# Negated decay sums as the exponential's bias, two directions added ahead of one product, and z and turned outputs in two PSUM banks

## The reference

```python
A_cum = jnp.cumsum(A, axis=-1)
scores = jnp.einsum("bclhn,bcshn->bhcls", Cc, Bc) * jnp.exp(segsum(A))
y_diag = jnp.einsum("bhcls,bcshp->bclhp", scores, xd)
...
y = (y_f + y_b).reshape(b, L, D_SSD)
y = rmsnorm(y * jax.nn.silu(z.astype(F32)), ssd_norm_w)
```

## Time and profile before

| | |
|---|---|
| runs shown | 953.66, 953.76, 956.06 us; median 953.76 |
| profiled execution, its own time | 954.61 us |
| its span, first to last instruction | 952.8 us |
| PE busy in the span | 855.1 us (90%) |
| DVE, POOL, ACT busy | 401.3, 210.1, 162.7 us |

### The profile page before, as it was taken

One profiled execution on the slowest core, in us unless ns is written; L12 is line 12 of the kernel. 1 busy time (PEld: TensorE's weight loads), 2 busy tenths in 40 slices (PEclk: granted clock), 3 DMA queues, 4 the chain that ended last, 5 costly groups with the idle time before them and its releaser, 6 DMA issues.

```text
span 952.8 us, 18676 instructions
## 1 busy us (share of the span) xinstructions
PE 855.1 (90%) x8036; PEld 483.1 (51%) x8036; DVE 401.3 (42%) x773; ACT 162.7 (17%) x369; POOL 210.1 (22%) x255
## 2 busy tenths in 40 slices
PE   1899999999899999999999994699998999999940
PEld 1656655555554555564444442455554555555520
DVE  1430012644664589985323265632222322222227
ACT  4121001212222222221010012011111111111113
POOL 0169999600141333330000000100000000000022
PEclk9999999999899999999999997699999999999985
DMA  9942755880310000069200004399999999998427
GB/s 349 419 171 90 274 223 212 290 312 1 133 44 1 1 1 1 0 239 337 115 22 23 9 14 147 142 381 419 390 415 397 352 401 379 406 404 334 152 75 279
DMA packets 41809, 198.91 MB, mean 209 GB/s; under 512 B 6848, under 2 KB 16256, under 8 KB 24704
## 3 DMA queue, kind: packets, MB, share of 16 engines
q1 hardware_dynamic: 22032, 162.82, 43.2%
q0 software_dynamic: 6224, 22.55, 6.8%
q10 hardware_dynamic: 13472, 12.37, 4.1%
HBM read 175.66 MB, written 22.05 MB: 208 GB/s over the span
## 4 chain that ended last, share of the span: by engine, by line
PE 57%; DVE 9%; DMA 3%; issue 2%; POOL 1%; ACT 1%; ACTq 0%; DVEq 0%; POOLq 0%
PE bank L928 19%; PE bank L796 14%; PE bank L941 9%; PE bank L660 6%; DMA slot_out<-yT 2%; PE bank L918 2%; PE bank L933 1%; PE bank L698 1%; DVE ex L1629 1%; DVE xs L1682 1%; DVE xs L2009 1%; POOL ex L1436 1%; DVE ex L1645 1%; PE bank L762 1%; DMA ex<-slot_out,ri 1%
## 5 line engine op out<-in xcount | busy, mean ns | idle before, releaser
L588 PE MATMUL bank<-hT,ring 128*128 128x512 f32 (+1 forms) x640 | 178.4, 438 | 1.5 <-DMA ring<-w_ring 1.5
L588 PEld LDWEIGHTS bank<-hT,ring 128*128 128x128 f32 x640 | 95.8, 192 | 72.0 <-issue 69.8
L1930 DVE TENSOR_TENSOR bcT<-bcT,bank 128x128 f32<-128x128 f32 x51 | 14.6, 287 | 166.4 <-ACT bcT L1255 166.4
L660 PE MATMUL bank<-ring,hT 128*128 128x512 f32 x160 | 76.9, 617 | 4.5 <-DVE ex L1653 2.2
L928 PE MATMUL bank<-ex,yT 128*32 128x256 f32 x1216 | 75.8, 392 | 1.2 <-ACT yT L1265 1.2
L928 PE MATMUL bank<-ring,yT 128*32 128x256 f32 x1248 | 76.5, 387 | 0.0
L796 PE MATMUL bank<-ring,yT 128*128 128x512 f32 x160 | 70.9, 593 | 0.8 <-DVE yT L1691 0.8
L1444 POOL DMA_INDIRECT yT<-h_dram,token_of x16 | 15.5, 969 | 237.2 <-PE bank L918 220.2
L1436 POOL TENSOR_TENSOR ex<-ex,dts 128x512 f32<-128x512 f32 x40 | 44.3, 1106 | 101.6 <-ACT ex L1167 101.5
L928 PEld LDWEIGHTS bank<-ex,yT 128*32 128x32 f32 x1216 | 37.6, 113 | 28.1 <-issue 3.4
L928 PEld LDWEIGHTS bank<-ring,yT 128*32 128x32 f32 x1248 | 38.4, 111 | 26.3 <-issue 2.2
(11 more groups left out here) (311 smaller groups left out, 1228.0 us busy)
## 6 DMA issues: line engine op xcount, KB each, us to landing
ex<-w_exp SPq DMA_DIRECT2D x36, 1024.0 KB, 18.0
ring<-w_exp SPq DMA_DIRECT2D x36, 1024.0 KB, 15.7
ring<-w_ring SPq DMA_DIRECT2D x13, 2048.0 KB, 11.6
yT<-w_late SPq DMA_DIRECT2D x16, 1024.0 KB, 6.6
hT<-w_exp SPq DMA_DIRECT2D x12, 1024.0 KB, 15.8
uT<-w_exp SPq DMA_DIRECT2D x12, 1024.0 KB, 18.2
slot_out<-ex POOLq DMA_DIRECT2D x13, 512.0 KB, 16.7
ex<-x SPq DMA_DIRECT2D x5, 512.0 KB, 8.3
```

What stands on the lines that cost most here:

```text
L588: mm = pe.matmul(o, w[:, k, (f % 4) * P:(f % 4 + 1) * P], hT[:, k, lo:hi], start=(k == 0), stop=(k == KT - 1))
L660: mm = pe.matmul(psb[6][:, :], hT[:, k, j * P:(j + 1) * P], w[:, k, :], start=(k == 0), stop=(k == KT - 1), skip_group_check=True)
L1930: tt(ab[v % 2], sg[v % 2], psb[v % 2][:, P:2 * P], ALU.mult).then_inc(s_ac, 1)
```

## The change

Three edits. The products of L741 go: instead, ten small products ahead of z of group 0 put all negated sums into bank 7, ACT copies them to `ncum`, and the exponential of each 128 columns takes its column of `ncum` as a per-partition bias, so that one exponential of 512 columns becomes four of 128. DVE adds the two directions first (256 columns) and multiplies the sum by C·B (256 columns). z of group jg goes to bank 6 or 7 by turns, and so do the turned outputs; z of group jg then waits for the silu of jg-2, or, from group 4 on, for the copy of the turned outputs of jg-4. `turn_y` of group jg moves behind `diagonal(4jg+7)`, into PE's step 4jg+10, and DVE's copy of it moves to behind its step 4jg+8. The first part of the output projection waits for the copies and the silus that used its bank.

```diff
--- before.py
+++ after.py
@@ -230,6 +230,14 @@
         def out_bank(j, hf_, c):
 
             return psb[6] if (j, hf_, c) == (0, 0, 1) else psb[2 * c + hf_]
+
+        def z_bank(jg):
+
+            return psb[6 + jg % 2]
+
+        def turn_bank(jg):
+
+            return psb[7] if jg >= 2 * NJ - 3 else psb[6 + jg % 2]
 
         def pooled_banks(i):
 
@@ -303,6 +311,7 @@
         s_sout = sem("context_states_stored")
         s_wd = sem("decays_times_dt")
         s_e = sem("exponents_built")
+        s_nc = sem("negated_sums_copied")
         s_ex = sem("decays_exponentiated")
         s_w = sem("scores_decayed")
         s_dg = sem("diagonal_products")
@@ -654,10 +663,14 @@
                 w = ring[:, m % RING, :].rearrange("p (k c) -> p k c", k=KT)
                 if ks[0] == 0 and jg < 2:
                     pe.wait_ge(s_ring[m % RING], 16 * (m // RING + 1))
-                if ks[0] == 0 and jg >= 1:
-                    pe.wait_ge(s_zs, jg)
+                if ks[0] == 0 and jg == 1:
+                    pe.wait_ge(s_nc, 1)
+                if ks[0] == 0 and 2 <= jg < 4:
+                    pe.wait_ge(s_zs, jg - 1)
+                if ks[0] == 0 and jg >= 4:
+                    pe.wait_ge(s_yT, jg - 3)
                 for k in ks:
-                    mm = pe.matmul(psb[6][:, :], hT[:, k, j * P:(j + 1) * P], w[:, k, :],
+                    mm = pe.matmul(z_bank(jg)[:, :], hT[:, k, j * P:(j + 1) * P], w[:, k, :],
                                    start=(k == 0), stop=(k == KT - 1), skip_group_check=True)
                 if ks[-1] == KT - 1:
                     mm.then_inc(s_z, 1)
@@ -726,6 +739,11 @@
                     pool_product(n + 2)
             pe.wait_ge(s_st, 5)
             pe.wait_ge(s_u, 8)
+            for d in range(2):
+                for j in range(NJ):
+                    c = j * 32 + d * H
+                    pe.matmul(psb[7][:, c:c + H], tabT[d][:, j * P:(j + 1) * P], nstackb[:, d * H:(d + 1) * H],
+                              start=True, stop=True)
             project_z(0, range(KT))
 
 
@@ -735,12 +753,6 @@
                 if i >= 2:
                     pe.wait_ge(s_ex, i - 1)
                 pe.matmul(o[:, :], idb[:, :], MASK4, start=True, stop=False, skip_group_check=True)
-                o4 = o[:, :].rearrange("p (h d t) -> p h d t", h=2, d=2)
-                for d in range(2):
-                    c = d * H + hh
-                    pe.matmul(o4[:, :, d, :], tabT[d][:, j * P:(j + 1) * P],
-                              nstackb[:, c:c + 2].unsqueeze(2).to_broadcast([96, 2, P]), start=False, stop=False,
-                              skip_group_check=True)
                 for q in range(4):
                     h, d = hh + q // 2, q % 2
                     c = d * H + h
@@ -775,11 +787,12 @@
 
             def turn_y(jg):
                 pe.wait_ge(s_yc, jg + 1)
-                if jg >= 1:
+                pe.wait_ge(s_zs, min(jg + 3, 2 * NJ))
+                if jg >= 2 * NJ - 2:
                     pe.wait_ge(s_yT, jg)
                 for q in range(4):
                     k = 4 * (jg % 2) + q
-                    mm = pe.transpose(psb[7][:, q * P:(q + 1) * P], xs[:, jg // 2, k * P:(k + 1) * P], ident)
+                    mm = pe.transpose(turn_bank(jg)[:, q * P:(q + 1) * P], xs[:, jg // 2, k * P:(k + 1) * P], ident)
                 mm.then_inc(s_ytr, 1)
 
 
@@ -809,14 +822,15 @@
                 if NS - 3 <= i < NS + 1:
 
                     if i == NS - 3:
-                        pe.wait_ge(s_zs, 2 * NJ)
+                        pe.wait_ge(s_zs, 2 * NJ - 1)
+                        pe.wait_ge(s_yT, 2 * NJ - 3)
                     project_part(0, 0, 1, range(2 * (i - NS + 3), 2 * (i - NS + 4)))
                 if i >= 3:
                     k = i - 3
                     diagonal(k)
                     if k % 4 == 0 and k // 4 >= 2:
                         from_states(k // 4)
-                    if k % 4 == 1 and k // 4 >= 1:
+                    if k % 4 == 3 and k // 4 >= 1:
                         turn_y(k // 4 - 1)
 
             pe.wait_ge(s_yp, 2 * NJ)
@@ -1157,15 +1171,18 @@
                 act.wait_ge(s_z, jg + 1)
                 if jg >= 3:
                     act.wait_ge(s_yc, jg - 2)
-                act.activation(zbuf[jg % 3], psb[6][:, :], ACT.Tanh, scale=0.5).then_inc(s_zt, 1)
+                act.activation(zbuf[jg % 3], z_bank(jg)[:, :], ACT.Tanh, scale=0.5).then_inc(s_zt, 1)
 
             def exps(i):
                 j, hh = i // HG, 2 * (i % HG)
                 act.wait_ge(s_e, i + 1)
                 if i >= WBUFS:
                     act.wait_ge(s_dg, i - WBUFS + 1)
-                act.activation(wbuf(i)[:, :, :, :], psb[4 + i % 2][:, :].rearrange("p (h d t) -> p h d t", h=2, d=2),
-                               ACT.Exp).then_inc(s_ex, 1)
+                for q in range(4):
+                    c = j * 32 + (q % 2) * H + hh + q // 2
+                    ins = act.activation(wbuf(i)[:, q // 2, q % 2, :], psb[4 + i % 2][:, q * P:(q + 1) * P], ACT.Exp,
+                                         bias=ncum[:, c:c + 1])
+                ins.then_inc(s_ex, 1)
 
             def square_y(jg):
                 act.wait_ge(s_yc, jg + 1)
@@ -1174,6 +1191,9 @@
                 act.activation(junk_y, xs[:, jg // 2, (jg % 2) * 512:(jg % 2 + 1) * 512], ACT.Square,
                                accum_out=stat[:, 16 + jg:17 + jg]).then_inc(s_ys, 1)
 
+            act.wait_ge(s_z, 1)
+            act.activation(ncum, psb[7][:, 0:160], ACT.Copy).then_inc(s_nc, 1)
+            act.wait_ge(s_nc, 1)
             tanh_z(0)
             for i in range(NJ * HG):
                 if i % 4 == 3 and i // 4 + 1 < 2 * NJ:
@@ -1642,15 +1662,14 @@
                 if i == 0:
                     dve.wait_ge(s_gs, 3)
                 w = wbuf(i)
-                step(tt(w.rearrange("p h d t -> p (h d) t"), w.rearrange("p h d t -> p (h d) t"),
-                        gT[:, j, hh // HG, :].unsqueeze(1).to_broadcast([P, 4, P]), ALU.mult))
-
-                tt(w[:, :, 0, :], w[:, :, 0, :], w[:, :, 1, :], ALU.add).then_inc(s_w, 1)
+                step(tt(w[:, :, 0, :], w[:, :, 0, :], w[:, :, 1, :], ALU.add))
+                tt(w[:, :, 0, :], w[:, :, 0, :], gT[:, j, hh // HG, :].unsqueeze(1).to_broadcast([P, 2, P]),
+                   ALU.mult).then_inc(s_w, 1)
 
             def silu_z(jg):
 
                 dve.wait_ge(s_zt, jg + 1)
-                stt(zbuf[jg % 3], zbuf[jg % 3], 1.0, psb[6][:, :], ALU.add, ALU.mult).then_inc(s_zs, 1)
+                stt(zbuf[jg % 3], zbuf[jg % 3], 1.0, z_bank(jg)[:, :], ALU.add, ALU.mult).then_inc(s_zs, 1)
 
             def per_head(ap):
                 return ap.unsqueeze(2).to_broadcast([P, HG, HD])
@@ -1688,7 +1707,7 @@
                     dve.wait_ge(s_sout, 32)
                 dve.wait_ge(s_ytr, jg + 1)
                 j, k = jg // 2, 4 * (jg % 2)
-                tt(yT[:, k:k + 4, j * P:(j + 1) * P], psb[7][:, :].rearrange("p (k t) -> p k t", k=4),
+                tt(yT[:, k:k + 4, j * P:(j + 1) * P], turn_bank(jg)[:, :].rearrange("p (k t) -> p k t", k=4),
                    vec[:, V_SN + k:V_SN + k + 4].unsqueeze(2).to_broadcast([P, 4, P]), ALU.mult).then_inc(s_yT, 1)
 
             silu_z(0)
@@ -1696,7 +1715,7 @@
                 if i % 4 == 3 and i // 4 + 1 < 2 * NJ:
                     silu_z(i // 4 + 1)
                 decay_scores(i)
-                if i % 4 == 1 and i >= 8:
+                if i % 4 == 0 and i >= 8:
                     copy_y(i // 4 - 2)
                 if i % 4 == 2 and i >= 4:
                     end_outputs(i // 4 - 1)
```

## The result

The changed kernel takes 941.65 us (median of 4 runs, 938.15 to 944.48) against 954.72 for the kernel before: a ratio of 0.986, 95% interval 0.982 to 0.990. In a second comparison, on another occasion, it was 940.24 against 954.67, 0.985 (0.983 to 0.987). Its profiled execution took 941.26 with a span of 939.4, so 13.4 less than the 952.8 of the earlier trace rows.

What follows compares the result with a forecast made beforehand. PE was taken as the bound, DVE only a little behind. Terms from z to z summed to −13.6 us, 954.61 to 941.0; with the median 0.85 below its profiled execution, 940.2 was forecast, range 936.5 to 945.0.

Steps and rivals of the forecast that it cites:

- ten products: Ahead of z of group 0, on PE's path: the small products building negated sums cost 0.4 us (bounds 0 and 1.0).
- group 0 to 1: Between these z starts: one exponent build less, and PE's idle 0.92 us falls to 0.25, together −0.9 us.
- 2 to 3: Between these z starts: four exponent builds less and PE's idle 1.98 us gone, together −2.9 us.
- 3 to 4: Between these z starts: four exponent builds, 0.37 us wait and the slow clock's 1.7 go, together −2.9 us.
- the five groups: The groups after z of group 4: each loses 0.88 us of exponent builds and 0.37 of wait, −6.25 in all.
- the end: Behind the last z, set by DVE: decays 1.3 us shorter, but silu 13.5 instead of 12.3 behind z; −0.1 (±1.6).
- L747's pace needs no cover: Four products behind the mask, each step: without L741 covering weight loads they keep 0.055 us each, 0.22 together.
- z's new wait stays empty: Ahead of z from group 4: the copy of four groups back has 3.0 us and takes 0.7, so PE doesn't wait.
- That is cover, not gain, as long as PE is in front: DVE in the 40 steps: 0.27 us less a step, 12.77 to 11.7, brings no gain while PE is in front.
- They may fall elsewhere: DVE's collisions with POOL, three of 0.85 us in a group: may move; no gain counted.
- The clock: Rival, chance 0.10: PE's idle ahead of 438.32 grows to 2 us or more, or group 3 stays slow; costs 1.7, 941.9.
- DVE as the bound: Rival, chance 0.07: collisions and standing still at its copy make groups 13.5 us; six lose 0.85 each, 945.3.

Runs made afterwards that it cites:

- the mask twice: Changed kernel with DVE's copy of turned outputs two steps later, plus each step's mask product made twice on PE: 945.02 us, ratio 0.990.
- the copy two steps later: Changed kernel with DVE's copy of the turned outputs behind step 4jg+10 instead of 4jg+8: 936.27 us, ratio 0.981; again 936.0, 0.981.
- one bank: Changed kernel without the banks edit: bias and DVE's order, one bank for z, turn and copy at old places: 944.5 us, ratio 0.990.

## Why the prediction was right

It forecast 940.2; the median is 941.65. Term by term, from the starts of z in the two profiled executions:

| term | forecast | measured |
|---|---|---|
| ten products | +0.4 | +0.26 |
| group 0 to 1 | −0.9 | −1.12 (8.72 to 7.60) |
| 1 to 2 | −0.9 | −1.09 (10.35 to 9.26) |
| 2 to 3 | −2.9 | −3.06 (13.48 to 10.42) |
| 3 to 4 | −2.9 | −2.98 (15.61 to 12.63) |
| the five groups | −6.25 | −6.08 (69.63 to 63.55) |
| the end | −0.1 | 0.0 |
| together | −13.6 | −14.1 |

Of the five groups, the one from 382.06 to 395.07 took 13.01, as PE there waits for its own z to give a buffer back. The span fell by 13.4: the ten products start 0.2 later than z of group 0 did before, and from the stage's end to the end of the span 0.5 was lost again. The ten products came cheaper than the pace of the earlier trace rows, which was read where the granted clock was 0.50 (593 to 594.5 us); here it was 1.00.

**Right and shown:** by experiment, that PE sets the pace of the groups (the mask twice, with the copy two steps later; the groups take 12.63 with either place of the copy); by the trace, that L747's pace needs no cover (in the changed kernel L759 starts at 394.85 and z behind it at 395.07, 0.22 for the four, and a group takes 12.63), that ACT's longer way is covered, that z's new wait stays empty, and that DVE's standing still doesn't reach PE inside the groups.

**Right as a sum, wrong in its parts:** the end. DVE's silu of group 9 came 14.5 behind z's start (409.56 − 395.07), not 13.5, against 12.3 before; from there to the last of L1689 took 14.8 (to 424.38), not 15.7, against 17.0 before. Both shifts were nearly twice what I worked out, and they cancel: that this term came right was luck.

**Mis-sized:** "That is cover, not gain, as long as PE is in front" for DVE's order. Taken back from the changed kernel it costs 0.2 in a group and 1.7 in the end, and alone it gives 6.2 us of stage, against nothing for the bias and 1.6 for the banks (7.9 with the copy two steps later). The step that gave it no gain was the one that left the collisions as they were ("They may fall elsewhere"). DVE's busy time in a group fell from 12.7 to 10.1, not to 11.7, as the collisions in it went from 2.5 us (L1645 1.54, L1648 1.25, L1682 1.55) to 1.0: the gating product lost its own, but a score product that starts behind POOL still takes 1.15 instead of 0.42:

```profile
355.55 1.07 POOL L1456 TENSOR_TENSOR ex<-ex,dts 128x512 f32<-128x512 f32 x1 [2.00 <-ACT ex L1183]
355.74 1.15 DVE L1666 TENSOR_TENSOR ex<-ex,gT 128x256 f32<-128x256 f32 x1
```

In the changed groups these cost PE nothing. The page GPSIMD Engine Reference of the Trainium skill, section 1 Specifications, has GpSimd share its SBUF interfaces with VectorE, with contention when VectorE's instruction has two SBUF inputs; the traces agree: in the kernel before, L1682 with two such inputs took 1.55 where it started behind L1436 (350.93) and 0.69 where it started ahead of it (406.61, L1436 at 406.95), and L1653, with one input in PSUM, took 0.69 with L1436 running all the while (407.33 to 408.02, L1436 from 406.95 to 408.20).

**The rivals.** The clock's condition came true, 2.26 us of idle time, and its price was paid in some executions only (below). Of the others none came: no group longer than 13.02, L759 at its old pace, ACT at 0.26 a column block, and nothing given back later beyond 0.5. The rivals that lie outside the range add up to 0.22, not 0.17: with 945.3, DVE as the bound is one of them. On ACT the estimate from the Trainium skill's page ScalarE: Activation LUTs, section What ACT_TABLE_LOAD costs, 1.27, was too high; the measurement, 1.14, decides.

## What to carry to other kernels

Where two engines are within a few per cent of each other, work taken from one is worth nothing until the wait on the other is gone: the bias alone gave 0, though the same work on PE is worth 0.87 us in a group where nothing else waits (the mask twice). When a producer moves later in one engine's order, move its consumer too: with the copy two steps too early the banks alone gave 0.2% and the whole change 1.4%, with the copy two steps later 0.8% and 1.9%, mended by one number. And read where the saved time of an engine lies in the chain, not its sum: 0.27 us less of DVE turned round which engine waits in a collision, and took 0.85 out of the chain.

## What the runs showed of the hardware

The same idle time did not always cost the clock. The changed kernel has 2.26 us of idle PE ahead of the second half of the output projection in both of its profiled executions. In the first the granted clock stayed at 1.00 and the 16 products and the turn took 8.35 (424.44 to 432.79). In the second (granted clock is the third column from the right):

```profile
426.00:428.00 2.00, 0.61 (x2) 0.38 (x3) 1.97 (x4) 0.00 (x0) 0.00 (x0) 1.00 1.01 336
428.00:430.00 2.00, 2.00 (x5) 0.93 (x4) 1.22 (x2) 0.71 (x2) 0.00 (x0) 0.70 0.83 348
430.00:432.00 2.00, 2.00 (x3) 0.67 (x2) 0.17 (x1) 1.69 (x4) 0.00 (x0) 0.50 0.96 328
```

There PE fell to 1.2 GHz and the same work took 10.05 (427.39 to 437.44), 1.7 more. Over all profiled executions, idle times of 2.05 to 2.40 at this place cost the clock in three of five and none of 1.47 or less did. Ahead of group 3, 1.83, 1.98 and 2.74 cost it (one bank, the kernel before, the bias alone) and 0.85 did not (DVE's order alone). So a wait of 2 us of PE can cost 1.7 us more than it looks. The spread of the whole time doesn't show it: the version two steps later ran from 933.65 to 939.59 in eleven runs, the changed kernel from 937.46 to 944.48 in nine.

Where an instruction of DVE with two inputs in SBUF met one of POOL, the one that started second took longer in the cases shown: DVE's gating product 1.55 instead of 0.69, or POOL's product 1.37 instead of 1.05, as shown with DVE's order alone.
